# Gathers of 32 tokens by four slots in sets of four, and a ring of two weight blocks in place of three

## The reference

```
s1, s2 = scores of the two halves of the query against 128 keys each
v1,i1 = top16(s1); v2,i2 = top16(s2)
sc,pos = top16(v1[:,None] + v2[None,:]); idx = i1*128 + i2 at pos
gate = softmax(sc)
act  = gate * gelu(t . u[idx])          # 128 dots per token
y    = sum over the 128 slots of act * v[idx]
```

## Time and profile before

| | |
|---|---|
| median of 3 runs | 1930.86 us |
| lowest, highest | 1923.73, 1937.14 us |
| profiled execution | 1922.51 us |
| its span, first to last instruction | 1920.7 us |
| mean granted TensorE clock | 0.88 |
| PE, DVE, ACT, POOL busy | 1527.7, 1334.4, 419.1, 584.6 us |
| moved by DMA | 703.32 MB, mean 366 GB/s |

### The profile page before, as it was taken

One profiled execution on the slowest core, in us unless ns is written; L12 is line 12 of the kernel. 1 busy time (PEld: TensorE's weight loads), 2 busy tenths in 40 slices (PEclk: granted clock), 3 DMA queues, 4 the chain that ended last, 5 costly groups with the idle time before them and its releaser, 6 DMA issues.

```text
span 1920.7 us, 22276 instructions
## 1 busy us (share of the span) xinstructions
PE 1527.7 (80%) x7828; PEld 920.6 (48%) x7828; DVE 1334.4 (69%) x3962; ACT 419.1 (22%) x1139; POOL 584.6 (30%) x551
## 2 busy tenths in 40 slices
PE   7999899776757979888889687998889875655555
PEld 7644675433213757656557265765656631111111
DVE  5767656868886779675445777877844579778655
ACT  1212201000002722622211264154120210000001
POOL 0011133344442322322322322232232244454441
PEclk9999799677677999999899899999999897776877
DMA  9888589999998977987999997699699999999995
GB/s 370 338 321 321 195 353 421 421 421 419 419 421 336 421 287 259 420 329 278 401 409 410 407 407 316 234 388 369 236 393 397 413 366 421 421 422 420 422 422 221
DMA packets 100255, 703.32 MB, mean 366 GB/s; under 512 B 15264, under 2 KB 15648, under 8 KB 16560
## 3 DMA queue, kind: packets, MB, share of 16 engines
q0 software_dynamic: 78336, 570.46, 73.6%
q1 hardware_dynamic: 21808, 131.45, 16.9%
HBM read 700.82 MB, written 1.05 MB: 365 GB/s over the span
## 4 chain that ended last, share of the span: by engine, by line
PE 39%; DMA 25%; DVE 16%; issue 5%; ACT 4%; POOL 1%; DVEq 0%; POOLq 0%; ACTq 0%
PE PS L1648 15%; DMA ub<-in_peer_uv,idx 10%; DMA vb<-in_peer_uv,idx 9%; PE PS L1798 3%; PE PS L2015 3%; PE PS L1991 3%; DMA ring<-in_peer_uv,idx 3%; PE PS L1704 2%; PE PS L1972 2%; DVE vb L1149 2%; DVE ub L1149 2%; DMA mods<-in_peer_uv,idx 2%; PE PS L1875 1%; DMA ring<-in_gdn_z 1%; PE PS L1893 1%
## 5 line engine op out<-in xcount | busy, mean ns | idle before, releaser
L1648 PE MATMUL PS<-ub,z 128*64 128x512 f32 x832 | 321.4, 752 | 110.6 <-DVE z L1115 110.4
L1648 PE MATMUL PS<-vb,z 128*64 128x512 f32 x816 | 309.2, 739 | 122.1 <-DVE z L1115 114.8
L2052 POOL DMA_INDIRECT ub<-in_peer_uv,idx x208 | 232.3, 1117 | 493.1 <-PE PS L1648 424.4
L2052 POOL DMA_INDIRECT vb<-in_peer_uv,idx x204 | 218.2, 1070 | 469.4 <-PE PS L1648 419.3
L1361 ACT ACTIVATE tanhs<-cubed 128x2 f32<-128x2 f32 x256 | 52.0, 203 | 872.2 <-DVE cubed L1104 871.2
L1648 PEld LDWEIGHTS PS<-vb,z 128*64 128x64 f32 x816 | 71.5, 158 | 267.7 <-DVE z L1115 173.2
L1648 PEld LDWEIGHTS PS<-ub,z 128*64 128x64 f32 x832 | 74.4, 161 | 260.8 <-DVE z L1115 166.2
L1149 DVE CUSTOM_DVE_ANT_0 ub<-ub,h 128x1024 f32<-128x1024 f32 x104 | 127.1, 1222 | 46.6 <-DMA ub<-in_peer_uv,idx 45.7
L1149 DVE CUSTOM_DVE_ANT_0 vb<-vb,h 128x1024 f32<-128x1024 f32 x102 | 124.8, 1223 | 39.6 <-DMA vb<-in_peer_uv,idx 38.9
L1108 DVE SCALAR_TENSOR_TENSOR acts<-tanhs,gated_x 128x2 f32<-128x2 f32 x256 | 40.6, 159 | 152.6 <-ACT tanhs L1361 152.5
L1648 PE MATMUL PS<-mods,z 128*64 128x512 f32 x208 | 125.9, 736 | 23.3 <-DVE z L1115 23.0
(11 more groups left out here) (364 smaller groups left out, 2800.9 us busy)
## 6 DMA issues: line engine op xcount, KB each, us to landing
ring<-in_gdn_qkv SPq DMA_DIRECT2D x32, 1024.0 KB, 9.7
ring<-in_peer_wq SPq DMA_DIRECT2D x23, 1024.0 KB, 9.9
two_slots<-in_ada_wide POOLq DMA_DIRECT2D x20, 1024.0 KB, 6.3
ring<-in_gdn_z SPq DMA_DIRECT2D x16, 1024.0 KB, 9.8
ring<-in_gdn_w_out SPq DMA_DIRECT2D x16, 1024.0 KB, 9.4
ring<-in_gla_w_in SPq DMA_DIRECT2D x6, 2048.0 KB, 9.4
mods<-in_ada_wide POOLq DMA_DIRECT2D x11, 1024.0 KB, 6.6
ring<-in_ada_w SPq DMA_DIRECT2D x4, 2048.0 KB, 11.8
```

The lines of the kernel that those rows point to most:

```text
L1648: last = pe.matmul(y[64 * g:64 * g + 64, e, :], z[:, i % 4, g, :], rows[:, D + e * 512:D + (e + 1) * 512], start=False, stop=False, skip_g ...
L2052: pool.indirect_dma_start(row_buffers[b], None, uv_rows, off).then_inc(row_landed[b].sem, 16)
```

## The change

A gather holds 32 tokens by four slots. A set is four gathers, g = 0 to 3, one for each quarter of the tokens. The activations, the `tanh`, the weight and the spread are made once for four gathers (tiles of 128x4 in place of 128x2; `z` is still 128x128). TensorE sums a set by eight products, of which each gives 32 rows of `y`. `by_quarter` writes indices and gates by 16 small instructions each, where `by_half` took four. h is spread by token quarter, four times over the partitions; quarter 3 goes to `h[:, w % 2]`, quarters 0 to 2 have one place each (`mods`, `vb` and a new tile `third`), so that they are copied only after the stretch before has spread its last weights. In every stretch they are made by products of 128 columns. The ring has two slots; the third is row buffer 9, so that there are 12 buffers and 10 in the middle stretches. Due times of the steps that look ahead from a set move with it.

```
-        ra & (P // 2 - 1), spot [P, P // 2]
+        ra & (P // 4 - 1), spot [P, P // 4]
...
-            return n if n < 4 else n % 3
+            return n if n < 4 else n % 2
...
-                sp.wait_ge(g_used.sem, n - 2)
+                sp.wait_ge(g_used.sem, n - 3 if n < 6 else n - 1)
...
-            row_buffers += [mods[:, 0:2, :]...] + [area[...] for i in (1, 2)]
-            h_lower = [mods[:, 6, :], vb[:, 8, :]]
+            row_buffers += [mods[:, 0:2, :]..., ring_flat[:, 2 * 2048:3 * 2048]] + [area[...] for i in (1, 2)]
+            third = sb(scr, "third", [P, D])
+            h_quarters = [mods[:, 6, :], vb[:, 8, :], third[:]]
+            Q = P // 4
...
+            QUARTERS = (3, 0, 1, 2)
...
-                    free = range(11 if n // STRETCH in (0, 3) else 9)
+                    free = range(12 if n // STRETCH in (0, 3) else 10)
...
-                        for s in range(2):
-                            for g in range(2):
+                        for s in range(4):
+                            for g in range(4):
...   (indices and gates)
-                                if g:
-                                    ... spread_weight(i - 1, weighed); gelu_argument(i, dotted)
-                                elif n:
-                                    weighed = weight(i - 1)
+                                if g == 3:
+                                    gelu_argument(i, v_chain.next())
+                                elif g == 0 and n:
+                                    weighed = weight(i - 1)
+                                elif g == 1 and n > 1:
+                                    spread_weight(i - 1, weighed)
...
+                    def quarter_out(w, g):                      # ScalarE
+                        n = QUARTERS.index(g)
+                        if w and g < 3:
+                            act.wait_ge(z_ready.sem, z_ready.at(w * STRETCH // 4))
+                        for e in range(2):
+                            act.wait_ge(h_twice.sem, h_twice.at(8 * w + 2 * n + e + 1))
+                            to = h[:, w % 2, :] if g == 3 else h_quarters[g]
+                            act.activation(to[:, e * 512:(e + 1) * 512], PS[:, banks_of(w, g)[e], :], ACT.Copy)...
...
-                                    for g in range(2):
-                                        rows = row_buffers[row_turn[2 * i + g][0]]
-                                        last = pe.matmul(y[64 * g:64 * g + 64, e, :], z[:, i % 4, g, :], rows[...], ...)
+                                    for g in range(4):
+                                        rows = row_buffers[row_turn[4 * i + g][0]]
+                                        last = pe.matmul(y[Q * g:Q * g + Q, e, :], z[:, i % 4, g, :], rows[...], ...)
...
+                    def quarter(w, g):                          # TensorE
+                        ht = hTm[:, :, Q * g:Q * g + Q] if w >= 2 else hT[:, :, w * P + Q * g:w * P + Q * g + Q]
+                        if g in (1, 2) and w == 0 or g == 1:
+                            pe.wait_ge(h_ready.sem, h_ready.at(8 * w + (2 if g == 1 else 4)))
+                        if g == 2 and w:
+                            pe.wait_ge(ffn_gate.sem, ffn_gate.at(w))
+                        for e in range(2):
+                            for j in range(4):
+                                for s in range(4):
+                                    last = pe.matmul(PS[Q * s:Q * s + Q, banks_of(w, g)[e], j * P:(j + 1) * P], ht[:, 4 * e + j, :], ident[:], ...)
+                            last.then_inc(h_twice.sem, 1)
...
+                            if n == 11:                         # GpSimd
+                                pool.wait_ge(g_used.sem, 3)
```

## The result

| kernel | median us (lowest to highest) | span of the profiled execution |
|---|---|---|
| before | 1927.3 (1919.5 to 1937.1) | 1920.7 |
| changed | 1995.2 (1992.6 to 1995.6) | 1993.1 |

The ratio is 1.0355, with a 95% interval from 1.0318 to 1.0393: 68 us slower, where 7 us faster was forecast, and above the upper end of the range (1978).

What follows compares the result with a forecast made beforehand. DMA was taken to bound most of the kernel, leaving bandwidth unused at 218 to 260 us and in convolution and core. Middle stretches -28+13+3+2+3 = -7 us, twice -14; start +6, tail +1: -7 from 1930.9, 1924 us; range 1868 to 1978.

Steps and rivals of the forecast that it cites:

- The ring of two weight blocks: Middle stretches: two slots make blocks 5.35 us apart, 0.8 more; z and out 5 us each, queries 3: +13 us a stretch.
- the 7 us: Assumed landing of a weight block: 2.5 us at full rate, doubled for the gathers' queue beside it, plus 2.2 us.
- The convolution's blocks: Weight blocks of the delta net's convolution, further apart than the others: the two-slot ring was to cost 0 there.
- the ring binds: Rival, chance 0.12: z, out and query blocks cost 2.2 us more each at a landing of 9.7 us; 1987 us.
- Products of a set: Gather products on TensorE: four run at once, a set of four costs 1.86 us; -28 us a middle stretch (10 to 38).
- The 20 us of 700 to 900 us: Convolution and core of the delta net: of 25.6 us of PE time removed, 20 us were to become time.
- the last sentence of the prediction: Warned of a landing other than 7 us, or the 700 to 900 us gain meeting a VectorE and TensorE chain.
- Sets of four hold buffers longer: Middle stretches: ten buffers freed by fours hold on average, DMA may briefly run dry; +3 us a stretch (0 to 10).
- VectorE: Whole kernel: 56 us lighter, busy time near 1280 us, counted at nothing because it isn't the bound anywhere.
- h by quarters: Spreading h takes 256 instructions instead of 64, 7.3 us if four run at once; +2 us before stretches 2 and 3 each.
- The start: Before 260 us: h's quarters, first routing and later first buffer release delay gathers, gather 7 at 247 to 250 us; +6 us.
- Stretches 0 and 3: 260 to 600 us and from 1590 us on, as long as their DMA bytes: forecast unchanged in length.

## Why the prediction was wrong

**The ring of two weight blocks** is the step that failed: +13 us a stretch was forecast, and it is +36 in the kernel before and +40 with sets of four. By stages, with the ring alone: z +8.4 and out +9.2 (5 each forecast), query +9.6 (3 forecast), convolution and core +7.0 (0 forecast).

- The landing was taken as 7 us; its median on the chain is 8.1 us behind gathers by twos and 10.1 behind gathers by fours. The doubling in the 7 us was an estimate; the windows of the changed kernel above have the two queues at 53.1% and 46.6% for 6 us. The prediction's own (landing + 3.7) / 2 then gives 5.9 and 6.9 us a block. The z blocks of the changed kernel are 6.2 us apart in stretch 1 (5.3 forecast), those with the ring of two alone 5.3 and 5.8 in the two stretches.
- I had put the long median down to loads that queue two deep. The trace of the kernel before refutes it: in the middle stretches, loads asked for with no other load of the ring in flight have a median of 9.0 us (15 of them), with one in flight 9.7 (49), with two 10.7 (16). Most of the wait is there without any other load, and what the DMA engines move beside it is the gathers. The change itself puts more of them in the queue at once.
- The convolution's blocks were counted at nothing because they are further apart; PE waits 30.6 us for them in the changed kernel. The query blocks' stage grows by 18.9 us there.
- No step had the slower product after each wait (6.2 for 3.7 us). The granted clock is 0.82 over the z, out and query blocks, where it was 0.94.

The rival "the ring binds" had the stages of z, out and query and the landing of the changed kernel. Its condition, a landing from 8.5 us on, is met by all landings of the chain shown for the changed kernel, but not by those with the ring alone, which costs 36 us all the same. That its 1987 us come near is in part luck: it kept the 28 us for the products and had nothing for the convolution.

**Products of a set.** Four at once was right, 1.86 us a set, and so was the PE time removed: 34.8 us in conv and core, 38.4 forecast with 600 to 700 us. What it is worth was not: 28 us a stretch forecast, 13.7 measured with half the columns (VectorE as it was), and 11 by the table for all that sets of four bring. The 20 us of 700 to 900 us failed as the last sentence of the prediction feared: halving the dots gains as much as halving the products, so the stage isn't PE's alone. The granted clock fell too, to 0.90 over convolution and core from 0.93 and 0.97; what that costs there was not tried.

**Sets of four hold buffers longer.** +3 us forecast; +21.5 measured in the kernel before, with its nine buffers given back by fours. Its arithmetic (4.5 dots of 3.8 us against a landing of 10 to 14 us) was for an even spacing; GpSimd's waits of 8 to 22 us between bursts show that it isn't even. The tenth buffer of the change brings back 9 us of it (539.7 less 530.6).

The two go together, as the circle of 26 us shows: PE waits for a block, so a set's product waits behind it, its four buffers come late, and four gathers stand in front of the next load. A middle stretch, from the table: ring +36, return by fours +21, tenth buffer -9, the rest of sets of four -11 (500.2 less 510.9), +37 in sum against a measured +41. With both middle stretches (+82), the earlier start (-7) and the last stretch (-3) the span is 72 us longer, as the two profiled executions have it.

**VectorE.** "Near 1280 us" was wrong: its busy time stayed, 1334.8 us. The durations of its instructions add up to 57 us less, as forecast, but those removed ran beside one another (in the kernel before three of 0.15 to 0.16 us start within 0.19 us, from 656.06 us on), and the 16 writes of indices and of gates don't (2.9 us for 16, one behind another). Counting it at nothing was right.

**h by quarters** took more than forecast, 192 of its 256 instructions from 1084.76 to 1093.35 us where 5.5 us were forecast for them. Four at once holds (125 of them in 3.71 us); most of the excess is gaps between them, 1.9 us in all. It is all but hidden: cutting three quarters of it left the rest of the stretch as long. **The start** was right in its steps (gather 7 asked for at 247.4 us, forecast 247 to 250), yet stretch 1 began at 601.6 us, 7 us sooner than before, and not 6 later. The ring of two alone gives 601.3 and the return by fours 612.0; what sets this within these 11 us stays open. **Stretches 0 and 3** stayed to within some us (stretch 3 is 330 us for 333).

## What to carry to other kernels

Before taking a slot from a prefetch ring, ask what will be queued in front of its loads after the change, and on which other queue: a load shares the DMA engines with it, and its landing isn't a property of the load (here 4.8 us for a block asked for ahead of the gathers, a median of 8.1 us behind gathers by twos and 10.1 behind gathers by fours). When buffers are given back in larger batches, cost the latest one against the dots ahead of it, not the average. And where several engines pass a few buffers round, look for the step that returns them: one step of VectorE moved by one dot was worth 28 us, as much as all that sets of four gained here.

## What the hardware showed that I had not expected

Four products on different 32 columns of the array ran fully beside each other, with starts within 0.02 us: 8 products in the 1.86 us that 4 took with 64 columns, both at a granted clock of 1.00.

A cut of each load by partitions made landings half as long again to twice as long (15.2 and 20.6 us for 10), though the bytes and the row length stayed. Why it is so much, when the cut costs 2.1 us without gathers, isn't shown.

The DMA engines can look well used (0.83 of the time from 892 to 1081 us) while TensorE waits for a load: they are idle between bursts (912 to 914 us), because GpSimd can't ask before TensorE has used the buffers, and TensorE waits for the load.
